# A decoder layer on one core: the second token half's layer-norm scale computed by GpSimd, and a new order of ScalarE's work around it

## The reference

```
h = x @ w_in                       # split into q, k, v, z, gates, ...
o_a = gated_deltanet(...);  o_b = diff_attention(...)
merged = sigmoid(ga) * (o_a @ w_branch_a) + sigmoid(gb) * (o_b @ w_branch_b)
x = layer_norm(ALPHA * x + merged @ w_out, ln_g[0], ln_b[0])      # the first layer norm
ffn = (silu(x @ w_gate) * (x @ w_up)) @ w_down
x = layer_norm(ALPHA * x + ffn, ln_g[1], ln_b[1])
layer_norm(x) = (x - mu) * rsqrt(var + 1e-5) * g + b
```

## Time and profile before

| | us |
|---|---|
| median of 3 runs | 1946.66 (1946.53 to 1947.02) |
| the profiled execution | 1946.92 |
| its span, first to last instruction | 1945.1 |
| TensorE busy in the span | 1929.9 (99%) |
| VectorE busy | 1320.3 (68%) |
| ScalarE busy | 927.8 (48%) |
| GpSimd busy | 101.3 (5%) |

### The profile page before, as it was taken

One profiled execution on the slowest core, in us unless ns is written; L12 is line 12 of the kernel. 1 busy time (PEld: TensorE's weight loads), 2 busy tenths in 40 slices (PEclk: granted clock), 3 DMA queues, 4 the chain that ended last, 5 costly groups with the idle time before them and its releaser, 6 DMA issues.

```text
span 1945.1 us, 33020 instructions
## 1 busy us (share of the span) xinstructions
PE 1929.9 (99%) x11196; PEld 1587.2 (82%) x11196; DVE 1320.3 (68%) x1857; ACT 927.8 (48%) x1270; POOL 101.3 (5%) x296
## 2 busy tenths in 40 slices
PE   9999999999999999999999999999999999999997
PEld 7788887888888888888888888888888888888886
DVE  7768677676857777776566656577775466664656
ACT  5555465554445554545544445644443444443442
POOL 0102010010101111111000000000000000000000
PEclk9999999999999999999999999999999999999999
DMA  7444444444555555455565676555566565555555
GB/s 262 157 141 152 149 142 139 150 158 135 186 183 162 187 159 190 160 189 171 186 194 194 216 243 202 172 194 194 191 193 194 194 194 194 196 193 193 191 191 174
DMA packets 98014, 353.21 MB, mean 182 GB/s; under 512 B 10832, under 2 KB 11120, under 8 KB 97776
## 3 DMA queue, kind: packets, MB, share of 16 engines
q1 hardware_dynamic: 97904, 351.65, 55.1%
HBM read 349.51 MB, written 2.10 MB: 181 GB/s over the span
## 4 chain that ended last, share of the span: by engine, by line
PE 95%; DVE 2%; ACT 1%; DMA 1%; issue 1%; SPq 0%; DVEq 0%; ACTq 0%
PE pg L396 88%; PE B L396 5%; DMA raw<-in_weights 1%; DVE gates L1212 1%; PE B L494 0%; DVE wlo L1204 0%; PE B L668 0%; ACT whi L811 0%; PE B L585 0%; DVE cT L1212 0%; PE B L526 0%; PE B L677 0%; PE B L630 0%; PE B L639 0%; ACT hraw L1086 0%
## 5 line engine op out<-in xcount | busy, mean ns | idle before, releaser
L1204 DVE TENSOR_TENSOR wlo<-raw,whi 128x1024 fp32r<-128x1024 f32 (+1 forms) x640 | 779.3, 1221 | 493.1 <-ACT whi L811 475.6
L811 ACT ACTIVATE whi<-raw 128x1024 fp32r<-128x1024 f32 (+1 forms) x640 | 674.3, 1056 | 696.7 <-PE pg L396 684.0
L396 PE MATMUL pg<-whi,act_x 128*128 128x512 f32 x2960 | 951.2, 395 | 1.1 <-issue 0.5
L396 PEld LDWEIGHTS pg<-whi,act_x 128*128 128x128 f32 x2960 | 555.9, 188 | 123.7 <-issue 8.8
L396 PE MATMUL pg<-wlo,act_x 128*128 128x512 f32 x1480 | 574.7, 390 | 0.0
L396 PE MATMUL pg<-whi,act_a 128*128 128x512 f32 x1632 | 505.0, 389 | 0.5 <-DVE act_a L1204 0.3
L396 PEld LDWEIGHTS pg<-whi,act_a 128*128 128x128 f32 x1632 | 306.3, 188 | 64.9 <-DVE act_a L1204 1.3
L396 PEld LDWEIGHTS pg<-wlo,act_x 128*128 128x128 f32 x1480 | 278.3, 188 | 53.6
L396 PE MATMUL pg<-wlo,act_a 128*128 128x512 f32 x816 | 317.4, 389 | 0.0
L396 PEld LDWEIGHTS pg<-wlo,act_a 128*128 128x128 f32 x816 | 153.2, 188 | 31.7
L396 PE MATMUL pg<-whi,act_b 128*128 128x512 f32 x512 | 158.5, 389 | 0.0
(11 more groups left out here) (228 smaller groups left out, 1067.3 us busy)
## 6 DMA issues: line engine op xcount, KB each, us to landing
raw<-in_weights SPq DMA_DIRECT2D x646, 512.0 KB, 4.0
gates<-in_ln_in SPq DMA_DIRECT2D x4, 512.0 KB, 6.2
gates<-in_ln_in SPq DMA_DIRECT2D x1, 2048.0 KB, 8.6
out<-gates SPq DMA_DIRECT2D x8, 256.0 KB, 2.7
raw<-in_weights SPq DMA_DIRECT2D x4, 256.0 KB, 4.4
cT<-in_xT SPq DMA_DIRECT2D x2, 512.0 KB, 6.8
qT<-in_xrow SPq DMA_DIRECT2D x2, 512.0 KB, 7.0
kT<-in_xrow SPq DMA_DIRECT2D x2, 512.0 KB, 5.5
```

Source lines behind the costliest of these rows:

```text
L396: return nc.tensor.matmul(o, l, r, start=start, stop=stop)
L811: return nc.scalar.activation(o, i, ACT.Copy, scale=scale)
L1204: return V.tensor_tensor(o, a, b, op)
```

## The change

GpSimd takes over the three Newton steps and the shift of half 1: it waits for a new semaphore `dve_seed`, which VectorE raises after the seed, and runs `root` and two more instructions, the last of which raises `act_var`. VectorE drops its ten instructions for them. ScalarE's list is reordered: `round_x1(0, 3)` comes ahead of the rounding of weight tile 6, `round_x1(1, 0)` ahead of `normalize(0, 1, 1)`, and `round_x1(1, 1)` ahead of `normalize(0, 1, 3)`. The rest of the diff adds the name of the semaphore.

```diff
@@ ScalarE
             for cq in range(1, 4):
                 gain_x1(0, cq)
-                split_ffn(cq + 3)
+                if cq < 3:
+                    split_ffn(cq + 3)
                 round_x1(0, cq)
+            split_ffn(6)
             normalize(0, 1, 0)
-            normalize(0, 1, 1)
             split_ffn(7)
             gain_x1(1, 0)
+            round_x1(1, 0)
+            normalize(0, 1, 1)
             normalize(0, 1, 2)
-            round_x1(1, 0)
             gain_x1(1, 1)
+            round_x1(1, 1)
             normalize(0, 1, 3)
-            round_x1(1, 1)
             for cq in range(2, 4):
@@ GpSimd
+            pool.wait_ge(N["dve_seed"], 1 + 1)
+            pool.wait_ge(N["act_var"], 1)
+            ch(root(sm[:, 59:60], sm[:, 57:58]))
+            k = half[:, 0:1]
+            ch(G.tensor_tensor(k, lnmv[:, 1, 0:1], sm[:, 59:60], ALU.mult))
+            G.tensor_scalar(sm[:, 61:62], k, -1.0, 0.0, ALU.mult, ALU.add).then_inc(N["act_var"], 1)
@@ VectorE
                 lnc(seed(sm[:, 58 + t:59 + t], sm[:, 56 + t:57 + t]))
+                if t == 1:
+                    dve.sem_inc(N["dve_seed"], 1)
@@ VectorE
             last_group(1)
             split_x1(0, 1)
-            newton(1)
-            newton(1)
             split_ffn(4)
             split_x1(0, 2)
-            newton(1)
-            shift(1)
             split_ffn(5)
             split_x1(0, 3)
             split_ffn(6)
```

More of the change, by code:

```diff
@@ L273, in build @@
             dve_qkT pe_s dve_s1 dve_mx act_exp dve_pd pe_pT act_pT pe_pv act_oss dve_oh2 pe_oT2
-            act_oT2 dve_oT2 dve_m pe_mT dve_turn act_mT dve_mT dve_qs pool_rs dve_ss pool_rinv dve_os pool_os pool_chain conv_chain build_chain scan_chain da_chain gain_chain""".split()
+            act_oT2 dve_oT2 dve_m pe_mT dve_turn act_mT dve_mT dve_qs pool_rs dve_ss pool_rinv dve_os pool_os dve_seed pool_chain conv_chain build_chain scan_chain da_chain gain_chain""".split()
         N = {n: sem(n) for n in once + counted}
```

## The result

The changed kernel took 1949.70 us (median of 20 runs, 1949.23 to 1952.05) against 1946.76 of the kernel before (20 runs, 1945.45 to 1947.85): 2.9 us more, a ratio of 1.0016 with a 95% interval of 1.0010 to 1.0022. It is slower by a real but very small amount, inside the 0.2% of the prediction (1949.8 was forecast). Its profiled execution took 1949.41 us with a span of 1947.4.

A forecast was written before the change was run, and what follows sets the result against it. TensorE runs unbroken behind the passage, so shifts there reach the end one for one. Lost 2.4 + 1.9, won back 0.53 + 0.1 + 0.50, gives +3.1 us on the 1946.66 median: 1949.8, range 1946.9 to 1951.0.

The forecast's parts named there:

- GpSimd's chain ends: Fourteen GpSimd instructions for half 1's scale, each waiting for the last, would run from about 1213.73 to 1221.48 us.
- stretched GpSimd instructions: Six of GpSimd's fourteen would start under a VectorE subtraction and end about 0.05 us behind it.
- sum against before: Half 1's tile 0 on TensorE would start at 1227.90 instead of 1224.77 us: +3.1 us.
- The 128 x 512 subtraction: VectorE's smaller subtraction, seen in no row beside GpSimd, was treated as holding GpSimd like the 128 x 1024 one.
- its second case: GpSimd hardly held, 0 or 1 instruction: +0.6 us, 1947.2; chance 0.17.
- The rival of a chain hardly held: GpSimd held for 0 or 1 instruction, only the transposes (1,1) waiting, 1.7 lost: +0.6 us, 1947.2; chance 0.17.
- the first wait: TensorE's transposes of chunk (1,0) wait for normalize(0, 1, 0), which GpSimd's chain releases: 2.4 us lost.
- the second wait: TensorE's transposes (1,1) wait for normalize(0, 1, 1), now behind chunk (1,0)'s gain and rounding: 1.9 us lost, however fast GpSimd.
- The rival of a chain held more: GpSimd's chain meets two more subtractions, VectorE's start up to 0.2 later; chain end 1222.5: +4.1 us, 1950.8; chance 0.11.
- The best case: Both 0.5 us stalls go and no turn waits: -1.15 us, 1945.5; chance 0.03.
- both stalls: TensorE's stalls at half 0's tile 5 (0.53 us) and half 1's tile 0 (0.50 us) would go.
- The clock rival: TensorE's clock falls after the two pauses; half speed over two or three tiles costs 3 to 4 us: 1953.5; chance 0.07.

The follow-up runs named there:

- e7: The changed kernel with 160 more small GpSimd instructions, on a number nobody reads, behind the first feed-forward group: 1950.10 us against 1947.10 for the kernel before.
- e1: The kernel before with only ScalarE's new order, the Newton steps staying on VectorE: 1948.16 us against 1947.11 for the kernel before.
- e4: The changed kernel with one Newton step instead of three on GpSimd, half 1's scale less exact: 1947.36 us against 1947.11 for the kernel before.
- e5: The changed kernel with six Newton steps instead of three on GpSimd: 1953.73 us against 1947.10 for the kernel before.

## Why the prediction was right

The mechanism was right, in both of its waits: all steps are found in the trace, counted from VectorE's seed of half 1 (1213.43 in the prediction, 1212.89 measured).

| step | predicted | measured |
|---|---|---|
| GpSimd's chain ends | 8.05 | 7.75 |
| stretched GpSimd instructions | 6 (1, 2, 5, 6, 8, 10) | 6 (2, 3, 6, 7, 9, 11) |
| transposes (1,0) start; lost there | 8.96; 2.4 | 8.65; 2.0 |
| transposes (1,1) start; lost there | 12.65; 1.9 | 12.35; 1.9 |
| half 1's tile 0 starts | 14.47 | 14.23 |
| sum against before | +3.1 | +2.9 |

- The small excess, 0.3 us, is in the chain of GpSimd. Its first instruction got through before the first subtraction, because the semaphore instruction put that one at 0.31 behind the seed instead of 0.19; every later one moved up by one place, which leaves three free ones at the end of the chain and not four. That the time came within 0.1 us of the forecast is in part luck: the rise was forecast 0.2 too high (3.1 against 2.94), and the forecast started from the median of 3 runs, 1946.66, where 20 runs give 1946.76.
- The 128 x 512 subtraction, which no row of before showed beside GpSimd, holds it as the 128 x 1024 one does (0.51, 0.55 and 0.57). With e7 this is what the Trainium skill, page "SBUF — State Buffer", section "Who interferes with whom", says of VectorE instructions with two SBUF inputs and of GpSimd reading SBUF; the trace agrees, with 1.24 against 0.19. The prediction says that without this rule its sum would be its second case; that isn't so. By its own step-through, with the 128 x 512 ones holding nothing, three instructions instead of six are held, the chain ends some 0.8 us earlier and the rise is about 2.3 us (an estimate), which is neither of its two rivals on GpSimd.
- That the order has its own wait, independent of GpSimd, is shown by e1 (1.58 with the Newton steps on VectorE) and e4 (1.56 with a short chain).
- The rival of a chain hardly held fell as well: unheld, by the distances here (0.29 to the start, 13 x 0.275, 0.19 for the last), the fourteen would have ended about 4.1 us after the seed, an estimate, and ScalarE was free for the normalization only at 5.62 (1218.51). So, by this estimate, the stretching is the whole of the first wait. Its sum is borne out by e4, whose short chain leaves the second wait alone: +0.75 against its +0.6.
- The rival of a chain held more fell: it was held as often as counted. The best case fell too: both stalls went, as it said, but each turn waited.
- The clock rival did not come in the changed kernel, with a granted 1.00 through pauses of 1.84 and 1.66; e5 shows that it was a real one, and that a pause of 5.10 us brings it about. Its price in the prediction (3 to 4 us, 1953.5) is not tested by that. e5 pays 1.1 us, because its slow matmuls of tile 6 fill a pause that is there anyway; the prediction's case, a clock that falls after the second pause, would have had no further pause to fill, and no run here shows it.
- The span shows +2.3 and not +2.9, because the passage began 0.54 us earlier in that execution; the medians of 20 runs, +2.94, agree with D.

## What to carry to other kernels

A chain of small instructions moved from a busy VectorE to an idle GpSimd is not free. It is slowed by the very work for which it made room, one GpSimd instruction held for each VectorE instruction with two SBUF operands: here ten VectorE instructions of 0.16 us, done 4.4 us after the seed with other work between them, became fourteen on GpSimd, done 7.75 us after it. When an in-order list is reordered to have one result earlier, look at what was done in a pair: the second of the pair may be wanted soon, by an engine whose own last result is needed by what now stands between them. Here TensorE had 1.9 us of work between the two sets of transposes and ScalarE's list 3.7 us between the two normalizations; the difference was paid with a slow chain on GpSimd (1.66 idle) and with a fast one (1.56) alike.

## What the runs showed of the hardware that was not expected

- Two pauses of TensorE, 1.84 and 1.66 us with 2.0 us of work between, left the granted clock at 1.00; one of 5.10 us brought it to 0.50, where it stayed for over 5 us after TensorE went on, and four transposes then took 0.77 us to the next instruction instead of 0.42.
- Four transposes that follow a pause take 0.42 us to the next instruction (1221.54 to 1221.96); in the running stream they take 0.35 (1220.63 to 1220.98).
- A GpSimd instruction of 0.19 us that was already running when VectorE's subtraction began (1213.18 against 1213.20) delayed the subtraction by little: it shows 0.72 us instead of the 0.69 of its like. It is so in all six kernels with the Newton steps on GpSimd, and 0.69 in the three without.
- Each VectorE instruction with two SBUF operands held one GpSimd instruction and no more, over 37 of them (e7). That it matters that GpSimd reads SBUF is not tested: all its instructions here do.
